# Expert items: tokens gathered by one-hot products in the loop, and twelve chunk homes in one order

## What is computed

```python
def moe_swiglu(h, router, wg, wu, wd):
    logits = jnp.einsum('td,de->te', ht, router).astype(jnp.float32)
    top_vals, top_idx = lax.top_k(logits, TOP_K)          # 2 of 8 experts for each token
    gates = jax.nn.softmax(top_vals, axis=-1)
    ...
    for e in range(N_EXPERTS):
        out = out + dense_gate[:, e:e + 1] * swiglu(ht, wg[e], wu[e], wd[e])
```

## Time and profile before

| | us |
|---|---|
| median of 3 runs | 1341.54 |
| the profiled execution | 1342.61 |
| its span | 1340.8 |
| item 0 on TensorE | 399.73 to 485.75 |
| item 1 (64 places) | 485.75 to 551.02, with 58.49 busy |
| items 2 to 6 | 551.02 to 979.44, with 427.81 busy |
| last item (64 places) | 979.44 to 1065.41, with 61.01 busy |

### The profile page before, as it was taken

The page is one execution under the profiler, slowest core; times in us unless marked ns, Lnnn a source line. Parts: engine busy times, 40 slices in busy tenths (PEclk is TensorE's granted clock), DMA queues, the critical chain, the costliest instruction groups (busy, mean ns, idle before and its releaser), DMA issues.

```text
span 1340.8 us, 30808 instructions
## 1 busy us (share of the span) xinstructions
PE 1287.3 (96%) x13911; PEld 888.5 (66%) x13911; DVE 566.2 (42%) x895; ACT 379.0 (28%) x509; POOL 78.1 (6%) x131
## 2 busy tenths in 40 slices
PE   8999999999999999899999999999986799999998
PEld 7879999889784454445445465554532388798896
DVE  7976545449953403004030040210401275647656
ACT  6665344344631000000100001000000256645643
POOL 3400000024101000000000000000001020000000
PEclk9999999999989999999999999999999999999999
DMA  9668885437499999999999999999999764333351
GB/s 320 189 220 281 287 275 205 153 113 232 153 356 374 424 422 425 422 423 423 423 422 422 423 422 424 424 421 424 423 422 424 305 224 134 119 126 127 98 188 61
DMA packets 92115, 407.33 MB, mean 304 GB/s; under 512 B 7443, under 2 KB 35843, under 8 KB 67410
## 3 DMA queue, kind: packets, MB, share of 16 engines
q1 hardware_dynamic: 83568, 390.22, 74.7%
q0 software_dynamic: 5408, 12.52, 2.9%
q10 hardware_dynamic: 3010, 2.63, 0.6%
HBM read 397.25 MB, written 16.12 MB: 308 GB/s over the span
## 4 chain that ended last, share of the span: by engine, by line
PE 74%; DMA 12%; DVE 10%; ACT 2%; issue 1%; DVEq 0%; SPq 0%; ACTq 0%
PE ps L2761 38%; PE ps L541 7%; PE ps L543 7%; PE ps L542 7%; DMA ering<-in_moe_wd 4%; DMA ering<-in_moe_wu 4%; DMA ering<-in_moe_wg 4%; DVE yT L2090 3%; PE ps L1236 2%; DVE low L531 2%; PE ps L1237 2%; PE ps L1238 2%; PE ps L1453 1%; PE ps L1455 1%; PE ps L1454 1%
## 5 line engine op out<-in xcount | busy, mean ns | idle before, releaser
L2761 PE MATMUL ps<-ering,xe 128*32 128x384 f32 (+1 forms) x5408 | 405.3, 460 | 19.0 <-DMA ering<-in_moe_wu 10.2
L2761 PEld LDWEIGHTS ps<-ering,xe 128*32 128x32 f32 x5408 | 178.4, 110 | 243.6 <-issue 134.0
L2761 PE MATMUL ps<-ering,eT 128*32 128x256 f32 x3728 | 205.4, 379 | 13.4 <-DMA ering<-in_moe_wd 13.4
L2268 DVE TENSOR_TENSOR eh<-eh,ps 128x384 f32<-128x384 f32 (+1 forms) x44 | 21.4, 487 | 439.2 <-PE ps L2761 439.2
L2761 PEld LDWEIGHTS ps<-ering,eT 128*32 128x32 f32 x3728 | 124.0, 110 | 94.5 <-DMA ering<-in_moe_wd 18.0
L531 DVE TENSOR_TENSOR low<-raw,high 128x2048 fp32r<-128x2048 f32 (+3 forms) x48 | 128.9, 2685 | 66.4 <-ACT high L526 65.2
L526 ACT ACTIVATE high<-raw 128x2048 fp32r<-128x2048 f32 (+3 forms) x47 | 105.5, 2244 | 93.1 <-PE ps L543 76.2
L541 PE MATMUL ps<-high,xT_hi 128*128 128x352 f32 (+1 forms) x368 | 128.2, 348 | 1.2 <-DVE xT_lo L2172 1.2
L543 PE MATMUL ps<-high,xT_lo 128*128 128x352 f32 (+1 forms) x368 | 127.2, 346 | 0.0
L542 PE MATMUL ps<-low,xT_hi 128*128 128x352 f32 (+1 forms) x368 | 126.8, 345 | 0.0
L1959 ACT ACTIVATE eo<-ps 128x512 f32<-128x512 f32 x6 | 3.6, 597 | 340.6 <-PE ps L2761 340.6
(11 more groups left out here) (449 smaller groups left out, 1683.0 us busy)
## 6 DMA issues: line engine op xcount, KB each, us to landing
ering<-in_moe_wg SPq DMA_DIRECT2D x62, 1408.0 KB, 22.1
ering<-in_moe_wu SPq DMA_DIRECT2D x60, 1408.0 KB, 24.0
ering<-in_moe_wd SPq DMA_DIRECT2D x46, 1536.0 KB, 24.9
rawb<-in_w_in SPq DMA_DIRECT2D x25, 1024.0 KB, 5.2
raw<-in_w_in SPq DMA_DIRECT2D x16, 1024.0 KB, 8.7
ering<-in_moe_wd SPq DMA_DIRECT2D x16, 1024.0 KB, 23.8
raw<-in_ffn_wg SPq DMA_DIRECT2D x8, 1408.0 KB, 6.6
raw<-in_ffn_wu SPq DMA_DIRECT2D x8, 1408.0 KB, 6.9
```

The lines of the kernel that those rows point to most:

```text
L2761: mm = nc.tensor.matmul(out_of(rows), tokens, columns_of(s), start=begins, stop=ends, skip_group_check=True)
```

## The change

- **Tokens.** `xs`, `xg`, the zero fills of `xs`, GpSimd's scatter and `load_tokens` are gone. VectorE makes the next item's one-hot matrix at the start of each item (`pick_next`: `row_of` less 96 places for each item, compared with a running index, for both of a token's rows), TensorE gathers after down chunk 17 into banks 0 to 2 (those of the gates), and VectorE turns the result straight from PSUM into `xe`. `xn`, `pick` and `row_of` stay in place through the loop for this.
- **Homes.** There are twelve in one order for every item: the eight slots of `ering`, `home_e` and `home_f` over arrays that the mixer has done with, `home_y` and `home_x` where `aside_y` and `aside_x` were. The last item leaves out `home_y`, which holds the `y` rows by then.
- **Places.** `eo`, `drop`, `eT`, `eh` and `pick_last` move; the waits at the beginning of the second block follow the new homes. There are still two items of 64 places.

```diff
-SMALL_ITEM, SMALL_TOKS = 1, 2
-RING2 = 10
+SMALL_ITEMS, SMALL_TOKS = (1,), 2
+HOMES = 12
...
     x = place("x", [P, NB, D], F32)
     over_xT = [at[0]]
-    aside = [nc.alloc_sbuf_tensor_at("aside_y", [P, 1, SLOT], F32, offset=ring_at + ESLOTS * SLOT * 4),
-             nc.alloc_sbuf_tensor_at("aside_x", [P, 1, SLOT], F32, offset=at[0])]
+    home_y, home_x = (nc.alloc_sbuf_tensor_at(n, [P, 1, SLOT], F32, offset=o) for n, o in (
+        ("home_y", ring_at + ESLOTS * SLOT * 4), ("home_x", at[0])))
+    pick_last = nc.alloc_sbuf_tensor_at("pick_last", [P, SMALL_TOKS, NB, P], F32, offset=at[0] + SLOT * 4)
     xT_hi = place("xT_hi", [P, KT, T], F32R)
     xT_lo = place("xT_lo", [P, KT, T], F32R)
...
-    LEAD = RING2
-
-    def in_ten(i):
-        return isinstance(i, int) and i < 2
-
-    def home(i, j):
-
-        if not in_ten(i):
-            return ering, j % ESLOTS
-        h = (FFN_CHUNKS * i + j) % RING2
-        return (ering, h) if h < ESLOTS else (aside[h - ESLOTS], 0)
-
-    def landing(i, j):
-        h = (FFN_CHUNKS * i + j) % RING2 if in_ten(i) else j % ESLOTS
-        return e_landed[h] if h < ESLOTS else aside_landed[h - ESLOTS]
-
...
+    SLOTS_OF = ((ering, 0), (ering, 1), (ering, 2), (ering, 3), (ering, 4), (ering, 7), (home_e, 0), (home_f, 0), (ering, 5), (home_y, 0),
+                (ering, 6), (home_x, 0))
...
+    LAST_HOMES = (0, 1, 2, 3, 4, 5, 6, 7, 8, 10, 11, 0, 1, 2, 3, 4, 5, 6, 7, 8, 10, 11, 5, 6)
+
+    def home_of(j, last):
+        return LAST_HOMES[j] if last else j % HOMES
...
+    def used_before(i, j, last=False):
+
+        if last:
+            users = [n for n in range(j) if LAST_HOMES[n] == LAST_HOMES[j]]
+            return chunk(i, users[-1] + 1 if users else LAST_HOMES[j] - HOMES + 1)
+        return chunk(i, j - HOMES + 1)
...
                         c += 1
                         if 4 <= j < 4 + ITEMS:
                             zero = a["c_zero"][0:1, :].to_broadcast([CAP, D])
-                            sp.dma_start(xs_rows[j - 4, :, :], zero).then_inc(zero_landed, 16)
                             sp.dma_start(ys_rows[j - 4, :, :], zero).then_inc(zero_landed, 16)
-                        if j == 4 + ITEMS:
-                            sp.dma_start(xs[ITEMS * CAP:, :], a["c_zero"][0:1, :].to_broadcast([P - CAP, D])).then_inc(zero_landed, 16)
-
-            def load_tokens(i):
-
-                if is_first(i):
-                    sp.wait_ge(xs_landed, 16 * 2 * NB)
-                    sp.wait_ge(g0_filled, 3)
-                else:
-                    sp.wait_ge(tp_freed, FREED * i)
-                first = (i + 1) * CAP
-                sp.dma_start(xg[:, :], xs[first:first + P, :] if isinstance(i, int) else xs[bass.ds(first, P), :]).then_inc(xg_landed, 16)
 
             def load_item(i, e, last=False):
                 for j in range(FFN_CHUNKS):
-                    if j == 12 and not last:
-                        load_tokens(i)
-                    sp.wait_ge(w_used, chunk(i, j - (RING2 if in_ten(i) else ESLOTS) + 1))
-                    load_expert(sp, i, e, j)
+                    sp.wait_ge(w_used, used_before(i, j, last))
+                    load_expert(sp, i, e, j, last)
 
             def expert_of(i):
                 at = slice(ORDER_COL + i, ORDER_COL + i + 1) if isinstance(i, int) else bass.ds(i + ORDER_COL, 1)
                 return sp.value_load(plan[0:1, at], min_val=0, max_val=NE - 1)
 
             for j in range(FFN_CHUNKS):
-                if j == 22:
-                    load_tokens(0)
                 if j < RAWS:
                     sp.wait_ge(lo_made, MOE0 - RAWS + j + 1)
-                elif j < ESLOTS:
-                    sp.wait_ge(w_used, MOE0 - SPLITS + (1, 2, 3, 1)[j - RAWS])
-                elif j == ESLOTS:
-                    sp.wait_ge(w_used, MOE0 - SPLITS + 2)
-                elif j < LEAD:
+                elif j in (6, 7):
+                    sp.wait_ge(cat_lo, 8)
+                elif j < HOMES - 1:
+                    sp.wait_ge(w_used, MOE0 - SPLITS + {4: 1, 5: 1, 8: 2, 9: 2, 10: 3}[j])
+                elif j == HOMES - 1:
                     sp.wait_ge(logits_ready, 1)
                 else:
-                    sp.wait_ge(w_used, chunk(0, j - LEAD + 1))
+                    sp.wait_ge(w_used, used_before(0, j))
                 load_expert(sp, 0, 0, j)
             sp.wait_ge(routed, 1)
-            load_item(1, expert_of(1))
-            with sp.Fori(2, NE - 1) as i:
+            with sp.Fori(1, NE - 1) as i:
                 load_item(i, expert_of(i))
             last = sp.value_load(plan[0:1, LAST_COL:LAST_COL + 1], min_val=NE - 1, max_val=ITEMS - 1)
             with sp.If(last > NE - 1):
...
             load_gain(4, a["norm_final"].rearrange("(o d) -> o d", o=1))
             pool.wait_ge(rows_made, 1)
-            pool.wait_ge(zero_landed, 16 * (2 * ITEMS + 1))
-            for r in range(2):
-                for b in range(NB):
-                    pool.indirect_dma_start(xs, bass.IndirectOffsetOnAxis(row_idx[:, r, b:b + 1], 0),
...
-            act.wait_ge(zero_landed, 16 * (2 * ITEMS + 1))
-            for i in range(SMALL_ITEM + 2):
+            act.wait_ge(zero_landed, 16 * ITEMS)
+            act.wait_ge(pick_made, PICKS_BEFORE)
...
                 if last:
                     add_rows(0)
                     add_rows(1)
+                if not last:
+                    pick_next(i)
                 if first:
-                    dve.wait_ge(xs_landed, 16 * 2 * NB)
                     dve.wait_ge(g0_filled, 4)
                     nc.vector.tensor_copy(drop[:, :, :, :].rearrange("p t b n -> p (t b n)"), ps[:, 6, :]).then_inc(g0_freed, 1)
                 hidden(i, 0, last)
...
                     add_rows(3)
                     return
                 dve.wait_ge(w_used, chunk(i, 15) + 1)
-                dve.wait_ge(xg_landed, 16 * (i + 1))
                 for t in range(TOKS):
-                    for s in range(STRIPS):
-                        rows = xg[STRIP * t:STRIP * t + STRIP, DOWN_N * s:DOWN_N * s + DOWN_N]
-                        nc.vector.transpose(xe[STRIP * s:STRIP * s + STRIP, :, STRIP * t:STRIP * t + STRIP],
-                                            rows.rearrange("p (c k) -> p k c", k=KT)).then_inc(tp_freed, 1)
+                    dve.wait_ge(g0_filled, 4 + TOKS * i + t + 1)
+                    turn_tokens(t, ps[:, t, 0:DOWN_N], tp_freed)
+
+            def pick_next(i):
+
+                before = PICKS_BEFORE + PICKS * i
+                rows = row_of if is_first(i) else rows_from
+                nc.vector.tensor_scalar(rows_from[:, :, :], rows[:, :, :], -float(CAP), None, ALU.add).then_inc(pick_made, 1)
+                dve.wait_ge(pick_made, before + 1)
+                for b in range(NB):
+                    nc.vector.tensor_scalar(pick[:, b, :], iota[:, 0:CAP], rows_from[:, 0, b:b + 1], None, ALU.is_equal).then_inc(pick_made, 1)
+                dve.wait_ge(pick_made, before + 1 + NB)
+                for b in range(NB):
+                    nc.vector.scalar_tensor_tensor(pick[:, b, :], iota[:, 0:CAP], rows_from[:, 1, b:b + 1], pick[:, b, :], ALU.is_equal,
+                                                   ALU.add).then_inc(pick_made, 1)
 
             def turn_tokens(t, rows, count):
                 nc.vector.transpose(xe[:, :, STRIP * t:STRIP * t + STRIP], rows.rearrange("p (c k) -> p k c", k=KT)).then_inc(count, 1)
...
                         pe.wait_ge(eo_made, 2 * i)
+                    if j == 18 and not last:
+                        pe.wait_ge(pick_made, PICKS_BEFORE + PICKS * (i + 1))
+                        for t in range(TOKS):
+                            gather(t, t)
...
             if c == RAWSB:
-                sp.wait_ge(w_used, chunk(n_items, 0) - 4)
+                sp.wait_ge(w_used, chunk(n_items, 0) - 3)
                 sp.dma_start(gain_b[:, :], a["norm_gain_2"][0:1, :].to_broadcast([P, D])).then_inc(gain_b_landed, 16)
             if c < RAWSB:
-                sp.wait_ge(w_used, chunk(n_items, 0) - (7, 6, 6)[c])
+                sp.wait_ge(w_used, chunk(n_items, 0) - (12, 11, 11)[c])
             else:
                 sp.wait_ge(blo_made, c - RAWSB + 1)
```

More of the change, by code:

```diff
@@ new lines, in model_program, with home @@
+    MIX_LANDED = 16 * MOE0 // RAWS
+    LANDED_OF = tuple((e_landed[s], MIX_LANDED) for s in range(RAWS)) + (
+        (e_landed[4], 0), (e_landed[7], 0), (ef_landed[0], 0), (ef_landed[1], 0), (e_landed[5], 0), (x_landed[0], 16),
+        (e_landed[6], 0), (x_landed[1], 16))
+    ROUNDS = FFN_CHUNKS // HOMES
+    LAST_HOMES = (0, 1, 2, 3, 4, 5, 6, 7, 8, 10, 11, 0, 1, 2, 3, 4, 5, 6, 7, 8, 10, 11, 5, 6)
+    def home_of(j, last):
+        return LAST_HOMES[j] if last else j % HOMES
+    def home(j, last=False):
+        return SLOTS_OF[home_of(j, last)]
@@ new lines, in landing, with landed @@
+    def landing(j, last=False):
+        return LANDED_OF[home_of(j, last)][0]
+    def landed(i, j, last=False):
```

(17 more changed lines are left out.)

79 lines of the change are left out of this document (34 added, 45 removed).

## The result

The changed kernel takes **1331.17 us** (median of 4 runs, 1330.31 to 1333.17) beside 1342.51 us (1340.18 to 1344.63) for the kernel before on the same chip: a ratio of 0.9918, with a 95% interval of 0.9897 to 0.9939. The forecast was 1324.4 us with a range of 1319 to 1331. The direction held. The gain is 11 us and not 17, and the time lies 0.17 us above the range. That much is less than the runs differ among themselves (1330.31 to 1333.17); the forecast missed by the 6 us of the gain.

The account below looks back on a forecast made before the run. TensorE was taken to bound the 96-place items and the weight stream the two of 64; 36.6 us of waits become 1.2, gathers cost 18.3, a gain of 17.1: from 1341.54 to 1324.4 us, range 1319 to 1331.

Parts of the forecast that it names:

- The gathers: Seven token gathers after down chunk 17 cost TensorE 2.61 us each, 18.3 us in all, with no waits.
- Removed traffic and closed holes: Weight stream loses 8.7 us of `xg` loads, 5.0 of scatters and 5.3 of holes before item 0's use: 19.0 us.
- Item 1: First item of 64 places: starts with ten chunks ready, keeps 10 us of lead less five, so no wait.
- Items 2 to 6: Items of 96 places: TensorE 88.2 us each, stream 82.7, so the lead grows 5.5 us an item, full by item 4.
- the lead at the last item's begin: Last item begins with nine or ten weight chunks ready; the other fourteen and `y` traffic take 53.7 us of stream.
- A tie, waits of 0 to 3 us, I take 1.2: Last item: final weights arrive 57 to 60 us after its begin, TensorE wants them at 57.0; 1.2 us of waits counted.
- The chain of `y` rows: End of last item: GpSimd's four gathers of `y` rows counted as zero cost, 1 to 3 us in the range.
- The small products: Down products of a 64-place item: 336 records at 0.0543 us, 18.2 us, making 56.3 with gates and ups.
- issue: Stretch at TensorE's jump into the last item, 2.6 us, kept in the sum of TensorE's own work.
- The sum: TensorE's end moves from 1065.4 to 1048.3: 36.6 us of waits become 1.2, 18.3 of gathers paid, 17.1 gained.
- the first rival: Stream stays the bound in the small items: 4 to 10 us of last-item waits return, 1328 to 1333 us; chance 0.15.
- an item of 64 places above 62 us: Sign that the forecast is wrong; the last item was forecast to take 59 to 61 us.

Follow-up runs that it names:

- run with the additions behind: Changed kernel with VectorE's first two additions of `y` rows moved behind the last item's hidden rows: 1329.37 us, ratio 0.9912 to the kernel before.
- gather-twice run: Changed kernel with each of the seven TensorE gathers in the loop done twice: 1349.58 us, ratio 1.0061 to the kernel before.
- without the gathers: Changed kernel without the seven loop gathers on TensorE and their turns on VectorE, output not the model's: 1326.27 us, ratio 0.9879 to the kernel before.
- three small items: Changed kernel with VectorE's two additions moved behind the hidden rows and item 2 also cut to 64 places: 1328.76 us, ratio 0.9907 to the kernel before.

## Why the prediction was right or wrong, point by point

- **The gathers: right.** 2.59 us each in the loop, 2.6 in the experiment with twice as many, against 2.61. Their waits for `pick` and for banks were zero, as forecast. The trace agrees here with what the prediction drew from the Trainium skill (TensorEngine Tiling, Tiling Modes) and not with four passes that nothing shares.
- **Removed traffic and closed holes: right.** 427 and 426 GB/s in the two windows that had 302 and 93; the item's stream is 423 GB/s, 422 in the row of before. The Trainium skill (DMA: Bandwidth & Descriptors, Where 436 GB/s comes from) gives about 358 GB/s as what binds a transfer from HBM to SBUF. The trace doesn't agree: 423 over 350 us. The Trainium skill (Perfetto Trace Analysis, Roofline) puts the ceiling of a core that has its memory to itself at some 435, which fits.
- **Item 1: right.** No wait. The lead was to be 10 less 5 us at its end; landings of up to 36 us say one or two chunks, 3 to 7 us. The extra homes fill; with two less, item 1 takes 3.4 us more.
- **Items 2 to 6: nearly right.** (988.31 - 548.91) / 5 = 87.88 us for 88.2. "The lead grows by 5.5 us an item" held: the stream moved 423 x 87.88 = 37.2 MB an item where 34.9 MB are used, 2.3 MB or 5.4 us. But **"is full by item 4" failed**, on the prediction's own numbers: 5 to 10 us and 5.5 an item reach 34 only at the end of item 6. The rate is 421 to 423 GB/s up to 965 us and first dips at the end of item 6, and loads there take 12 to 18 us and not 6 to 10.
- **The term that was mis-sized: the lead at the last item's begin.** The prediction put nine or ten chunks ready. Of the last item's 24 chunks 14 are issued after 988.31; of the ten before, three (issued at 975.7, 979.5 and 986.0, landing 14.8, 14.7 and 11.9 us later) are still under way: seven are ready. So 17 chunks are to come, not 14: 24.5 MB with `ys` and `y` rows on top, 27.0. In the run with the additions behind, 26.55 MB had been moved when the last one was there, 63.7 us after the item's begin at 417 GB/s, and not the 22.7 MB and 57 to 60 us of the forecast. "A tie, waits of 0 to 3 us, I take 1.2" became 6.9 us of waits for weights in that run, and in the changed kernel 6.1 for VectorE and 0.7 for a weight. What failed is the step before: a lead taken as full by item 4 that had barely reached its limit at the end of item 6. The count of ready chunks at a full lead was right. The gather-twice run, whose lead is full, starts its last item with nine ready, and by its landings the stream would then be some 2 us late, a tie as forecast.
- **The chain of `y` rows: wrong place.** The prediction looked at its end, where it costs nothing much (the last addition starts at 1050.97, ahead of the item's end). It overlooked that VectorE's order has additions 0 and 1 ahead of the hidden rows. In an item of 86 us they were through in time; in one of 66 us they are 6.1 us late. The 18 us until the chain starts did not shrink. Alone this costs as much as the stream: 6.89 us in the gather-twice run, 6.9 for the stream with the additions behind. Both together cost what the later of them does.
- **The small products.** A small item's down records number 352 (six chunks of 48, two of 32), not 336: 16 x 0.0543 = 0.9 us more in each of the two. Against it the 2.61 us of "issue" at the jump into the last item is gone, which the prediction had kept.
- **The sum.** Against the predicted end of the phase, 1048.3: item 0 starts 0.9 us later (less than one profile differs from another), item 1 takes 0.75 more, items 2 to 6 1.6 less, the "issue" 2.6 less, the last item 66.2 and not 57.5, 8.7 more. That is 6.2, and 1054.5 is where it ends. Of the 8.7, 5.6 are waits (6.8 for 1.2), 0.9 the records, 1.8 chunk 16 itself, which takes 4.36 us of path and not 2.6 (below), and the rest ends of products that nothing overlaps (1.93 us for the last chunk and not 1.7). It was luck that the missing "issue" and the faster items gave back 4.2 us: without them the kernel would take some 1335 us.
- **Rivals and range.** The time falls in the band of the first rival, the stream as the bound in the small items, with its 4 to 10 us and 1328 to 1333; the run with the additions behind shows that it holds, although the wait seen in the changed kernel is mostly VectorE's. It had 0.15. The prediction's own sign, "an item of 64 places above 62 us", came true for the last item (66.2 us). Since the tie was the weakest step, it deserved more, and a range that ended in its middle was too narrow by that.

## What to carry to other kernels

Where a stream and an engine take turns as the bound, the gain of an edit is read from the buffered lead at each turn, not from busy time: here two homes were worth 6.9 us and the two before them 15.2, while 18 us of TensorE's work were worth 2.5 us and 28 us were worth 1.5. Read the lead from the landing times and carry it item by item to the place where it is spent. When a stage gets shorter, go through the whole order of each engine in it for what stands ahead of the path's work, and ask of a wait that the profile names what would be late right behind it.

## What the runs showed of the hardware

- **A wait lowered TensorE's clock.** During the 6.11 us of waiting in the last item the granted clock fell to its lower level, 0.50 or 1.2 GHz, and 48 records took 4.36 us of path in place of 2.6. The windows of the changed kernel:

```profile
1025.00:1030.00 5.00, 1.36 (x20) 0.39 (x12) 0.30 (x1) 0.00 (x0) 0.00 (x0) 0.92 1.02 423
1030.00:1035.00 5.00, 2.53 (x24) 1.35 (x28) 4.83 (x8) 0.00 (x0) 1.57 (x2) 0.50 1.01 426
1035.00:1040.00 5.00, 5.00 (x88) 3.07 (x84) 1.02 (x2) 0.00 (x0) 0.00 (x0) 0.89 1.01 413
```

  With the same idle time in seven pieces of 0.2 to 1.8 us (additions behind) the clock stays at 1.00. The Trainium skill (TensorE: Matmul & The Clock Gate, What's actually happening) says that the clock has these two levels and that activity lifts it; both traces agree.
- **Gathers side by side land later.** The first two and the last two gathers of `y` rows take a median of 10.6 and 9.9 us to land one after the other, 12.0 and 19.1 us when all four are issued within 4.5 us.
- **The "issue" stretch at the jump into the last item** is 2.61 us before, absent in the changed kernel, 2.85 us without the gathers and 1.2 us with three small items. Why was not tried.
